# Attention scores as two matmuls over 128 rows, with the running sum kept in DRAM meanwhile

## The reference, cut to what matters

```
u = rms_norm(h, mix_norm)
q, k, v, pz, gates = split(u @ w_in)          # 12 heads of 64: 3 groups of 4
q, k = partial rope(q), partial rope(k)
# group g: window, dilation = (128, 1), (512, 4), (2048, 16)[g]
o_g, lse_g = softmax attention over the allowed keys of group g
o = sum_g softmax_g(lse_g) * o_g              # 4 heads of 64
h = h + (gates[0] * (o @ w_branch_attn) + gates[1] * (pool(pz) @ w_branch_pool)) @ w_out
```

## Time and profile before

| | |
|---|---|
| median of 3 runs | 1864.92 us (1864.58 to 1866.64) |
| the profiled execution, its own time | 1866.13 us |
| its span, first to last instruction | 1864.1 us |
| PE busy | 1850.0 us, 99% |
| DVE busy | 1324.1 us, 71% |
| ACT busy | 890.8 us, 48% |
| mean granted TensorE clock | 0.998 |
| the stage from `qk` of the first half to the end of `attend` of the second | about 360 to 540 us |

### The profile page before, as it was taken

How to read it: one execution, slowest core, us unless ns; L and a number is a source line. 1 busy time by engine, 2 the same in 40 slices (tenths; PEclk the granted TensorE clock), 3 DMA queues, 4 the chain that set the end, 5 groups by cost and what they waited for, 6 DMA issues and landing times.

```text
span 1864.1 us, 27146 instructions
## 1 busy us (share of the span) xinstructions
PE 1850.0 (99%) x10799; PEld 1627.6 (87%) x10799; DVE 1324.1 (71%) x1786; ACT 890.8 (48%) x1182; POOL 61.7 (3%) x80
## 2 busy tenths in 40 slices
PE   9999999999999999999999999999999999999997
PEld 7998998888889988989998888888888888888886
DVE  8875887887678889856888745463646776666666
ACT  6652664436365536634653342433336644444445
POOL 0000000010000000000000000000000000000000
PEclk9999999999999999999999999999999999999999
DMA  6744763341216426654753222122221222212213
GB/s 214 184 124 125 196 171 101 132 125 69 74 55 176 141 98 163 169 161 123 193 151 112 102 81 101 68 90 72 105 84 56 91 84 75 90 69 89 90 68 91
DMA packets 49633, 212.55 MB, mean 114 GB/s; under 512 B 5648, under 2 KB 8240, under 8 KB 38144
## 3 DMA queue, kind: packets, MB, share of 16 engines
q1 hardware_dynamic: 38816, 178.80, 28.1%
q0 software_dynamic: 10288, 31.84, 9.0%
q10 hardware_dynamic: 432, 0.56, 0.1%
HBM read 203.32 MB, written 3.67 MB: 111 GB/s over the span
## 4 chain that ended last, share of the span: by engine, by line
PE 94%; DVE 3%; ACT 1%; issue 1%; DMA 0%; DVEq 0%; ACTq 0%
PE acc L2419 20%; PE acc L2420 20%; PE acc L2421 20%; PE acc L2425 7%; PE acc L2426 7%; PE acc L2427 7%; PE att L2420 2%; PE att L2421 2%; PE att L2419 2%; PE att L2425 1%; PE att L2427 1%; PE att L2426 1%; PE acc L2683 1%; PE acc L2658 1%; DVE w_lo L1350 0%
## 5 line engine op out<-in xcount | busy, mean ns | idle before, releaser
L1350 DVE TENSOR_TENSOR w_lo<-raw,w_hi 128x2048 fp32r<-128x2048 f32 (+1 forms) x120 | 271.4, 2262 | 69.8 <-ACT w_hi L642 68.9
L642 ACT ACTIVATE w_hi<-raw 128x2048 fp32r<-128x2048 f32 (+1 forms) x120 | 226.5, 1888 | 120.4 <-PE acc L2421 105.6
L2419 PE MATMUL acc<-x_hi,w_hi 128*128 128x512 f32 x712 | 280.3, 394 | 0.3 <-DVE tmp L1578 0.3
L2421 PE MATMUL acc<-x_hi,w_lo 128*128 128x512 f32 x712 | 277.4, 390 | 0.0
L2420 PE MATMUL acc<-x_lo,w_hi 128*128 128x512 f32 x712 | 277.3, 389 | 0.0
L2419 PEld LDWEIGHTS acc<-x_hi,w_hi 128*128 128x128 f32 x712 | 133.7, 188 | 30.9 <-issue 2.7
L2420 PEld LDWEIGHTS acc<-x_lo,w_hi 128*128 128x128 f32 x712 | 133.7, 188 | 28.4 <-issue 1.2
L2421 PEld LDWEIGHTS acc<-x_hi,w_lo 128*128 128x128 f32 x712 | 133.6, 188 | 28.0
L2425 PE MATMUL acc<-xt_hi,w_hi 128*128 128x256 f32 x516 | 144.6, 280 | 0.0
L2427 PE MATMUL acc<-xt_hi,w_lo 128*128 128x256 f32 x516 | 144.3, 280 | 0.0
L2426 PE MATMUL acc<-xt_lo,w_hi 128*128 128x256 f32 x516 | 144.3, 280 | 0.0
(11 more groups left out here) (477 smaller groups left out, 4665.4 us busy)
## 6 DMA issues: line engine op xcount, KB each, us to landing
raw<-in_ret_head SPq DMA_DIRECT2D x24, 1024.0 KB, 4.8
raw<-in_ffn_down SPq DMA_DIRECT2D x32, 704.0 KB, 4.1
raw_c<-in_ffn_seven SPq DMA_DIRECT2D x37, 512.0 KB, 5.3
raw<-in_ffn_seven SPq DMA_DIRECT2D x33, 512.0 KB, 4.7
raw<-in_ffn_seven POOLq DMA_DIRECT2D x33, 512.0 KB, 7.5
raw<-in_ffn_seven SPq DMA_DIRECT2D x37, 256.0 KB, 4.5
raw<-in_ret_out SPq DMA_DIRECT2D x8, 1024.0 KB, 4.7
raw<-in_sb_v SPq DMA_DIRECT2D x8, 1024.0 KB, 4.7
```

Of the source, the lines that this page charges most:

```text
L642: nc.scalar.activation(w_hi[:, slot, at:at + cols], raw[:, slot, 0:cols], ACT.Copy).then_inc(w_hi_ready, 1)
L1350: tt(w_lo[:, slot, at:at + cols], raw[:, slot, 0:cols], w_hi[:, slot, at:at + cols].bitcast(F32), ALU.subtract).then_inc(w_ready, 1)
L2419: mm(dst, still[0], move[0], start=first, stop=False)
L2421: return mm(dst, still[1], move[0], start=False, stop=last)
```

## The change

Queries and keys of all three groups now get the form that group 0 had. `q_both` and `k_both` hold three groups, and the low part of the keys goes into new tiles `k_rest[j]`, in head j's own 64 rows, with zeros in the other 64. A score is then two matmuls over 128 rows for each group, with the same stationary operand: six instead of eight, beside the two that lay down the masks. `rope_done` writes the high part and the low part in two instructions of 64 rows for each group, not for group 0 alone. POOL issues twelve DMAs in each half instead of four, and `first_score` waits for all twelve.

The new tiles need room. `k_rest` and two of the three `q_low` tiles take the place of `h`, which SP writes to DRAM (2 MB, `h_parked`) once it is complete; DVE's first low part waits for that, and so does POOL, which clears the other rows of `k_rest` with two memsets. POOL reads `h` back in four DMAs of 512 KB behind the first four `add_pair` DMAs of the gates, and DVE waits for them before it adds `w_out`'s product. DVE's wait for the copies ahead of the pooling is gone.

The branch slab is split whole, in front of `mix_values(2, 0)` of the second half, no longer in quarters in units 0 to 3. The gate slab `mix_gate[0]`, which was split whole at the end of the second half (ACT behind unit 6, DVE behind unit 7), is split in quarters in units 4 to 7.

```diff
@@ -117,7 +117,11 @@
         sb("to_line", [P, P // 4])
+        with ExitStack() as under:
+            k_rest = [sb(f"k_rest{j}", [P, N_GROUPS, TOK], F32R, under) for j in range(2)]
+            q_low = [sb(f"q_low{g}", [P, TOK], F32R, under) for g in range(N_GROUPS - 1)]
         h = sb("h", [P, DC, TOK])
+        h_parked = nc.dram_tensor("h_parked", (P, DC, TOK), F32, kind="Internal").ap()
         raw = sb("raw", [P, RING, SLAB])
@@ -125,12 +129,9 @@
         x_lo = sb("x_lo", [P, DC, TOK], F32R)
-        with ExitStack() as under:
-            sb("tmp_first", [P, 4 * TOK], F32, under)
-            q_low = sb("q_low", [P, TOK], F32R, under)
         tmp = sb("tmp", [P, 6 * TOK])
         with ExitStack() as under:
-            k_low = sb("k_low", [P, TOK], F32R, under)
+            q_low.append(sb("q_low_last", [P, TOK], F32R, under))
         ssq = sb("ssq", [P, TOK])
@@ -250,10 +251,8 @@
             with ExitStack() as inner:
-                q_both = [sb(f"q_both{j}", [P, TOK], F32R, inner) for j in range(2)]
-                k_both = [sb(f"k_both{j}", [P, TOK], F32R, inner) for j in range(2)]
-                qk_hi = sb("qk_hi", [P, 2, N_GROUPS - 1, TOK], F32R, inner)
-                qk_lo = sb("qk_lo", [P, 2, N_GROUPS - 1, TOK], F32R, inner)
+                q_both = [sb(f"q_both{j}", [P, N_GROUPS, TOK], F32R, inner) for j in range(2)]
+                k_both = [sb(f"k_both{j}", [P, N_GROUPS, TOK], F32R, inner) for j in range(2)]
                 va = sb("va", [P, TB, N_GROUPS * GROUP_HEADS, 2, HEAD], F32R, inner)
@@ -490,6 +492,8 @@
                 fetch(dram["mix_qk"][0, g])
+            sp.wait_ge(h_ready, DC)
+            sp.dma_start(h_parked, h[:]).then_inc(park_landed, 16)
             for i in range(2):
@@ -585,15 +589,22 @@
+            pool.wait_ge(park_landed, 16)
+            pool.wait_ge(seg_done, FFN_SEGS[0] + 1)
+            for j, rows in enumerate(head_rows[::-1]):
+                nc.gpsimd.memset(k_rest[j][rows, :, :].bitcast(F32), 0.0).then_inc(rest_clear, 1)
+
             def other_halves(a):
                 own, other = head_rows, head_rows[::-1]
-                pool.wait_ge(both_ready, 2 * a + 1)
-                for j in range(2):
-                    pool.dma_start(q_both[j][other[j], :], q_low[own[j], :]).then_inc(both_landed, 16)
-                pool.wait_ge(both_ready, 2 * a + 2)
-                for j in range(2):
-                    pool.dma_start(k_both[j][other[j], :], k_both[j][own[j], :]).then_inc(both_landed, 16)
+                for g in range(N_GROUPS):
+                    done = 2 * (N_GROUPS * a + g)
+                    pool.wait_ge(both_ready, done + 1)
+                    for j in range(2):
+                        pool.dma_start(q_both[j][other[j], g, :], q_low[g][own[j], :]).then_inc(both_landed, 16)
+                    pool.wait_ge(both_ready, done + 2)
+                    for j in range(2):
+                        pool.dma_start(k_both[j][other[j], g, :], k_both[j][own[j], g, :]).then_inc(both_landed, 16)
@@ -609,6 +620,10 @@
                     v.next()
+                    if j < 3:
+                        pool.wait_ge(prob_ready, 2 * UNITS)
+                        rows = slice(2 * (2 * (j - 1) + k), 2 * (2 * (j - 1) + k) + 2)
+                        pool.dma_start(h[:, rows, :], h_parked[:, rows, :]).then_inc(h_back, 16)
@@ -868,11 +883,8 @@
                 act.wait_ge(val_ready, val.next())
-                if g:
-                    ins = nc.scalar.activation(qk_hi[:, o, g - 1, :], t(o), ACT.Copy, scale=QK_SCALE[o])
-                else:
-                    for j, rows in enumerate(head_rows):
-                        ins = nc.scalar.activation((k_both if o else q_both)[j][rows, :], t(o)[rows, :], ACT.Copy, scale=QK_SCALE[o])
+                for j, rows in enumerate(head_rows):
+                    ins = nc.scalar.activation((k_both if o else q_both)[j][rows, g, :], t(o)[rows, :], ACT.Copy, scale=QK_SCALE[o])
                 ins.then_inc(hi_ready, 1)
@@ -939,16 +951,15 @@
                 for k in range(UNITS):
-                    if k < PARTS:
-                        prep_part(k)
+                    part = k - a * (UNITS - PARTS)
+                    if 0 <= part < PARTS:
+                        prep_part(part)
                     if k + 1 < UNITS:
...
                         exps(k + 3)
-                    if a == 1 and k == UNITS - 2:
-                        prep()
@@ -984,6 +995,7 @@
             rope_done(N_GROUPS - 1, 1)
+            prep(12 * BLK)
             mix_values(2, 0)
@@ -1700,13 +1712,13 @@
                 dve.wait_ge(hi_ready, hi.next())
-                if g:
-                    stt(qk_lo[:, o, g - 1, :], t(o), QK_SCALE[o], qk_hi[:, o, g - 1, :].bitcast(F32), ALU.mult, ALU.subtract).then_inc(op_ready, 1)
-                else:
-                    for j, rows in enumerate(head_rows):
-                        stt((k_low if o else q_low)[rows, :], t(o)[rows, :], QK_SCALE[o], (k_both if o else q_both)[j][rows, :].bitcast(F32),
-                            ALU.mult, ALU.subtract).then_inc(both_ready if j else op_ready, 1)
-                    dve.wait_ge(both_ready, both.next())
+                if both.k == 0:
+                    dve.wait_ge(park_landed, 16)
+                for j, rows in enumerate(head_rows):
+                    dst, high = (k_rest[j][rows, g, :], k_both[j][rows, g, :]) if o else (q_low[g][rows, :], q_both[j][rows, g, :])
+                    stt(dst, t(o)[rows, :], QK_SCALE[o], high.bitcast(F32),
+                        ALU.mult, ALU.subtract).then_inc(both_ready if j else op_ready, 1)
+                dve.wait_ge(both_ready, both.next())
                 op.next()
@@ -1776,10 +1788,8 @@
                                             ALU.add).then_inc(acc_free, 2)
-                    if k < PARTS:
-                        prep_part(k)
-                if a == 1:
-                    prep()
+                    if 0 <= k - a * (UNITS - PARTS) < PARTS:
+                        prep_part(k - a * (UNITS - PARTS))
                 u.next(2 * UNITS)
@@ -1813,7 +1823,6 @@
             rope_done(N_GROUPS - 1, 1, 0)
-            dve.wait_ge(both_landed, 4 * 16)
             for i in range(4):
@@ -1988,6 +1998,7 @@
             sq.next()
+            dve.wait_ge(h_back, 4 * 16)
             with loop(dve, DC // 4, (n, 2), (s, 4), (u, 4), (step, 4), (sq, 4), (hi, 4), (op, 4)) as i:
@@ -2629,22 +2640,22 @@
             def scores(a, k):
-                r, rows = k // 2, slice(HEAD * (k % 2), HEAD * (k % 2) + HEAD)
+                r, head = divmod(k, 2)
                 if k >= 2:
...
                 b.next(2)
-                q = qk_hi[rows, 0, :, plain[r]], qk_lo[rows, 0, :, plain[r]]
-                both, keys = q_both[k % 2], k_both[k % 2]
                 mm(wide, ident_b[:], by_rows(band[:, DIL - 1 - r:2 * DIL - 1 - r, :]), start=True, stop=False)
                 mm(narrow[:, 0:2 * P], ident_b[:], by_rows(classes[:]), start=True, stop=False)
-                mm(wide, both[:, plain[r]], keys[:], start=False, stop=False)
-                mm(wide, both[rows, plain[r]], k_low[rows, :], start=False, stop=True)
-                for g in range(N_GROUPS - 1):
-                    last = passes(narrow[:, P * g:P * (g + 1)], (q[0][:, g, :], q[1][:, g, :]),
-                                  (qk_hi[rows, 1, g, plain[r]], qk_lo[rows, 1, g, plain[r]]), False, g == N_GROUPS - 2)
+                q, high, rest = q_both[head], k_both[head], k_rest[head]
+                mm(wide, q[:, 0, plain[r]], high[:, 0, :], start=False, stop=False)
+                mm(wide, q[:, 0, plain[r]], rest[:, 0, :], start=False, stop=True)
+                for g in range(1, N_GROUPS):
+                    dst = narrow[:, P * (g - 1):P * g]
+                    mm(dst, q[:, g, plain[r]], high[:, g, plain[r]], start=False, stop=False)
+                    last = mm(dst, q[:, g, plain[r]], rest[:, g, plain[r]], start=False, stop=g == N_GROUPS - 1)
                 last.then_inc(att_full, 2)
@@ -2705,7 +2716,8 @@
                 pe.wait_ge(op_ready, op.at())
-                pe.wait_ge(both_landed, 4 * 16 * (a + 1))
+                pe.wait_ge(rest_clear, 2)
+                pe.wait_ge(both_landed, 4 * N_GROUPS * 16 * (a + 1))
                 scores(a, 0)
```

More of the change, by code:

```diff
@@ L408, in block_kernel @@
         both_landed = sem("both_landed")
+        park_landed = sem("park_landed")
+        rest_clear = sem("rest_clear")
+        h_back = sem("h_back")
         mix_copied = sem("mix_copied")
```

## The result

The changed kernel takes 1880.63 us (median of 4 runs, 1880.29 to 1881.41), the kernel before 1865.29 beside it (1864.58 to 1866.64): ratio 1.0082, 95% interval 1.0065 to 1.0099. The forecast was 1874.0 with a range to 1879.5. The direction was right; the loss is 15.3 us where I had 9.15, and the time lies above the range.

A forecast was written before the change was run, and what follows sets the result against it. PE was taken to bound the kernel, with DVE lacking any lead at two spots. Value slab 4.8 plus second half's first score 8.5 (3.1 of it copies) minus gain 4.15 made 9.15 us over 1864.92: 1874.0, range 1869.0 to 1879.5.

The forecast's parts named there:

- What bounds the kernel: Whole kernel: PE, busy for 99% of the span, sets the time, but at two spots DVE has no lead.
- Both spots where DVE meets PE: First half's value slab and second half's first score: time added to DVE adds to the span, 4.8 and 5.4 us.
- The value slab: First half: longer DVE and ACT work moves the value slab from 407.3 to 412.1, PE waiting 4.8 us.
- The copies: Second half's first score: waits 3.1 us after the last low part for the key copies to be issued and land.
- The gain: PE's scores in attend: 1.34 instead of 1.71 us, 0.35 saved per counting unit, 4.15 us in all.
- all 8 count, 2.8: Second half's attend: all 8 units gain, 2.8 us, as ACT needs about 2.4 us a unit and PE 2.79.
- The clock: Rival, chance 0.16: PE's clock falls in the new waits, 2 us each; 1876.0 with one, 1878.0 with two.
- 1 to 3 us on the rotations: Second half's rotations: PE would show a new wait of 1 to 3 us.
- At nothing: Parking h and its return, memsets, moved copies: costed at zero; 2 to 6 us if a cover is gone.
- vector work covered: Rival, chance 0.13: DVE's added work fits where PE is not yet waiting; 1863.9, or 1858.9 with larger score gains.
- late transfers: Rival, chance 0.06: parked h or its return delays a slab or an add_pair, 2 to 6 us more.
- scores no shorter: Rival, chance 0.03: 128-row products of 128 columns have a pitch of 0.23, so the gain vanishes; 1878.1.

The follow-up runs named there:

- e2: Kernel before with the pairs of groups 1 and 2 written as two 64-row products on ACT and DVE, no copies, old scores: 1877.92 us.
- e3: Kernel before with every group's score as two 128-row matmuls, groups 1 and 2 reading group 0's operands: 1863.02 us, ratio 0.9984.
- e1: Changed kernel with matmuls that no result uses filling PE's three long waits: 1876.72 us.
- e4: Kernel before with only h written to DRAM and read back in four transfers: 1866.85 us, ratio 1.0005.
- e9: Changed kernel with the splits of the branch and gate slabs back at their old places: 1880.56 us.
- e13: Against kernel before: whole 128-row products, 16 transfers a half, group 2 keeping 64-row matmuls, each score's 128-row matmuls first: 1863.61 us, ratio 0.9989.
- e6: e5 with each transfer of keys released by ACT's write of that half, not by DVE's low parts: 1872.52 us.
- e5: Changed kernel with ACT's two 64-row halves passed to DVE one by one: 1872.79 us.
- e7: e6 with 10 matmuls that no result uses ahead of the second half's first score: 1870.29 us, ratio 1.0028.
- e10: Changed kernel with the last group's transfers of queries and keys reading the group before, which is ready earlier: 1877.73 us.
- e14: Kernel before with each score's wide 64-row matmul set between the two 128-row ones of bands and classes: 1868.99 us, ratio 1.0020.

## Why the prediction was wrong in its size

**What bounds the kernel.** Right. Both spots where DVE meets PE were real. I had 4.8 and 5.4 us for the two halves, 10.2. That e2's mark shows 10.9 is in part luck: its waits grew by 8.7 us, and the falls of the clock make up the rest.

**The value slab.** I had 4.8 us, the trace shows 5.1 (412.44 against 407.36). DVE's 64-row pairs have the forecast length, here in the second half:

```profile
506.32 1.41 DVE L1719 SCALAR_TENSOR_TENSOR q_low_last<-tmp,q_both 64x512 fp32r<-64x512 f32 x2 [1.33 <-ACT q_both L887]
...
512.31 1.41 DVE L1719 SCALAR_TENSOR_TENSOR k_rest<-tmp,k_both 64x512 fp32r<-64x512 f32 x2 [1.33 <-ACT k_both L887]
```

**The copies.** I had 3.1 us from the last low part to the score; it was 3.6, from 513.72 to the weight load at 517.30. The landing was as forecast (2.21 us, at 517.08). POOL's second issue came at 514.87, 0.86 behind the first and not 0.5, and 0.2 passed between landing and weight load. The last row is from the chain that ended last:

```profile
514.01 0.52 POOL L607 DMA_DIRECT2D k_both<-k_both  x1 [4.96 <-DVE k_rest L1719]
514.87 0.52 POOL L607 DMA_DIRECT2D k_both<-k_both  x1 [0.35 <-issue]
...
514.87 2.21 DMA k_both<-k_both
```

**The gain.** The score was forecast at 1.34 and lasts 1.20 where PE has not to wait:

```profile
533.51 0.39 PE L2650 MATMUL att<-band,ident_b 128*128 128x512 bf16 x1
533.74 0.27 PE L2651 MATMUL att<-classes,ident_b 128*128 128x256 bf16 x1
533.77 0.48 PE L2653 MATMUL att<-k_both,q_both 128*128 128x512 f32 x1
534.08 0.39 PE L2654 MATMUL att<-k_rest,q_both 128*128 128x512 f32 x1
534.31 0.22 PE L2657 MATMUL att<-k_both,q_both 128*128 128x128 f32 x1
...
534.60 0.27 PE L2658 MATMUL att<-k_rest,q_both 128*128 128x128 f32 x1
535.13 0.30 PE L2669 MATMUL acc<-ident,tmp 128*128 128x128 f32 x1 [0.26 <-DVE o_even L1789]
```

The last start, 534.60, and its pitch of 0.11 end it at 534.71. From classes to the second wide product it is 0.34, where I had carried over 0.43: in that lay 0.09 of the change to 64 rows, and the change back lay at the end (0.20 from 447.08 to 447.28, where the pitch is 0.11). So a score gives 0.5 and not 0.35. But only 3.0 of the forecast 4.15 us arrive (e3), about 1.2 for the 1.75 of the first half and 1.8 for the 2.4 of the second. 16 scores give 8.0; the three waits of e3 shown above and one of 0.7 for ACT's `tmp` sum to 4.1, 3.9 more than the kernel before has at these lines. That would leave 4.1, and I have not followed the remaining 1.1. The step that failed is the count of the units that gain, "all 8 count, 2.8" above all: I had checked ACT's 2.4 us a unit and left DVE out, which the trace names (`o_even`, 0.26 in the row above).

**The clock.** The step that failed most: the sum has no term for it. Each of the three long waits has half the clock in it or behind it (the windows above), and e1 prices the falls at 3.4 us. I had worked this rival out and gave it 0.16, against it only that "no wait inside the kernel is long enough to test it"; that is no evidence on either side. The Trainium skill ("TensorE: Matmul & The Clock Gate", section "HAM oscillation — how this bites in real kernels") says that waits for transfers bring the clock down, and that the next matmuls start at half of it. The trace agrees at the wait for the keys, where the score behind it starts at half clock (0.56 over 515 to 520), and shows the same behind two waits for DVE's writes. I counted two waits and there are three, since I had put 1 to 3 us on the rotations and the last one alone waits 3.3. My price of 2 us for a fall was fair (1.6 and 2.2 in e1).

**At nothing.** Parking h, its return, the order of the slabs: right (e4, e9). DVE shows no wait for the parked h, and behind 560 us the stage has its old length. The other three rivals fall: vector work covered by e2, late transfers by e4, scores no shorter by e3.

**The account at the mark:** 14.5 measured, 9.15 forecast, a gap of 5.3. The clock 3.4 (e1), the gain 1.15 too high (e3), the copies 0.5, the value slab 0.3: together 5.35. That the two meet so closely is luck, since each term comes from marks of single executions (the mark of e4 moved by 0.9 with nothing to show for it). These terms take the forecast from 1874.0 to 1879.4. The rest to 1880.63 lies outside them: the loss in time is 0.9 more than that at the mark, and the kernel before beside this run is 0.4 above the 1864.92 I started from.

## What to carry to other kernels

Before an engine that waits near zero gets work from a producer that has no idle time, price the work at full length, and where the new wait is as long as the ones here (3.0 to 4.4 us) add a fall of the clock, 1.6 to 2.7 us each here. A shorter instruction stream on TensorE gains only down to the next engine's unit time, so work out that time for every engine that serves the unit, not for one. Sort matmuls by row height before taking any away: e13, with the operands built by transfers, whole products on ACT and DVE and one going and coming per score, is the only version of the whole computation here that is below the kernel before by more than the noise, by 2.0 us (0.1%), and only just. Whether ACT or DVE could write the other 64 rows itself, without a transfer behind it, was not tried.

## What the runs showed of the hardware

All 14 waits of TensorE inside the kernel of 3.0 us or longer (3.0 to 4.4, in seven kernels; those for the keys are taken up to the weight load of the band) had the granted clock at half in them or right behind them. Shorter ones had it too, but not always: 2.22 us in e6 did, 2.24 in e5 and 2.27 in e7 at the same place did not, 1.54 in e10, with 0.95 close behind it, did. So equal waits can end differently.

Falls at one place can also cost different amounts. From the value slab to the first score of the first half it is 11.24 us where the clock stays up (e1, e5), 12.85 in the changed kernel and in e6, 13.55 in e10 and 13.91 in e9. So the fall there cost 1.6 to 2.7 us.

Going between matmuls of 128 and of 64 rows costs 0.15 to 0.20 us each, in the mean of going and coming (e13, e14).
